# Moving the MLP's input in four transfers per block and by tokens in fours, with three reorderings around it, in a seven-product fp32 trunk

## What is computed

```python
def gmlp_mixer(h, w_in, ln_g, w_s, b_s, w_out):
    z = jax.nn.gelu(h @ w_in)
    u, v = jnp.split(z, 2, axis=-1)
    ...  # v is layer-normed; ws is w_s below its diagonal, per group of 256 columns
    sv = jnp.einsum('gts,bnsge->bntge', ws, v) + b_s.T[None, None, :, :, None]
    return (u * sv.reshape(b, l, GM_WIDTH)) @ w_out

def channel_mlp(h, w1, w2):
    return jnp.square(jax.nn.relu(h @ w1)) @ w2

x = x + gmlp_mixer(rms_norm(x, norm1_g), ...)
x = x + channel_mlp(rms_norm(x, norm2_g), mlp_w1, mlp_w2)
return rms_norm(x, final_g)
```

## Time and profile before

| what | value |
|---|---|
| median of three runs | 1123.8 us |
| the profiled execution's own time | 1123.38 us |
| its span, first to last instruction | 1121.3 us |
| TensorE busy | 1110.0 us, 99% of the span |
| VectorE busy | 796.9 us (71%) |
| ScalarE busy | 563.3 us (50%) |
| DMA | 195.9 MB, mean 175 GB/s |
| granted clock of TensorE | 0.999 of full speed |

### The profile page before, as it was taken

One profiled execution on the slowest core, in us unless ns is written; L12 is line 12 of the kernel. 1 busy time (PEld: TensorE's weight loads), 2 busy tenths in 40 slices (PEclk: granted clock), 3 DMA queues, 4 the chain that ended last, 5 costly groups with the idle time before them and its releaser, 6 DMA issues.

```text
span 1121.3 us, 13104 instructions
## 1 busy us (share of the span) xinstructions
PE 1110.0 (99%) x5050; PEld 922.8 (82%) x5050; DVE 796.9 (71%) x872; ACT 563.3 (50%) x870; POOL 23.0 (2%) x17
## 2 busy tenths in 40 slices
PE   9999999999999999999999999999999999999997
PEld 7888888888888888888788888888888888888886
DVE  5885656689779986699858447455598575677666
ACT  7764344554554434644674455454644333333456
POOL 0000000000000000000000000000000000000240
PEclk9999999999999999999999999999999999999999
DMA  9072353272875594643353635527878354343213
GB/s 333 16 222 106 107 181 109 93 256 81 319 256 196 186 351 153 191 122 103 114 187 144 194 113 191 196 102 272 301 292 298 121 217 188 113 151 113 78 73 150
DMA packets 86541, 195.90 MB, mean 175 GB/s; under 512 B 5048, under 2 KB 15312, under 8 KB 79824
## 3 DMA queue, kind: packets, MB, share of 16 engines
q1 hardware_dynamic: 85168, 194.28, 49.6%
q10 hardware_dynamic: 1312, 0.79, 0.3%
HBM read 134.23 MB, written 58.72 MB: 172 GB/s over the span
## 4 chain that ended last, share of the span: by engine, by line
PE 89%; DVE 7%; ACT 2%; issue 1%; DMA 1%; SPq 0%; DVEq 0%; ACTq 0%
PE banks L438 29%; PE banks L443 29%; PE banks L442 29%; PE banks L531 3%; DVE ring_low L1426 1%; DVE raw_a L1522 1%; DVE left_and_right L1462 1%; DMA left_and_right<-in_a_w_in_dram 1%; ACT ring_high L990 0%; DVE rows L1589 0%; DVE rows L1568 0%; ACT raw_a L1039 0%; DVE s_low L1512 0%; DVE raw_s L1555 0%; DVE pair_low L1434 0%
## 5 line engine op out<-in xcount | busy, mean ns | idle before, releaser
L1020 ACT ACTIVATE pair_high<-left_and_right 128x1024 fp32r<-128x1024 f32 x168 | 177.2, 1060 | 247.4 <-PE banks L438 199.5
L1426 DVE TENSOR_TENSOR ring_low<-left_and_right,ring_high 128x512 fp32r<-128x512 f32 x224 | 153.1, 693 | 186.0 <-ACT ring_high L990 185.3
L1434 DVE TENSOR_TENSOR pair_low<-left_and_right,pair_high 128x1024 fp32r<-128x1024 f32 x168 | 204.3, 1231 | 111.2 <-ACT pair_high L1020 111.2
L990 ACT ACTIVATE ring_high<-left_and_right 128x512 fp32r<-128x512 f32 x224 | 138.0, 628 | 254.6 <-PE banks L438 155.9
L438 PE MATMUL banks<-pair_high 128*128 128x512 f32 x672 | 262.0, 390 | 0.0
L442 PE MATMUL banks<-pair_low,pair_high 128*128 128x512 f32 x672 | 261.7, 389 | 0.0
L443 PE MATMUL banks<-pair_high,pair_low 128*128 128x512 f32 x672 | 261.7, 389 | 0.0
L438 PE MATMUL banks<-s_high,ring_high 128*128 128x512 f32 x384 | 150.0, 391 | 2.9 <-DVE s_low L1512 2.1
L442 PE MATMUL banks<-s_low,ring_high 128*128 128x512 f32 x384 | 149.6, 390 | 0.0
L443 PE MATMUL banks<-s_high,ring_low 128*128 128x512 f32 x384 | 149.5, 389 | 0.0
L438 PEld LDWEIGHTS banks<-pair_high 128*128 128x128 f32 x672 | 126.2, 188 | 26.4 <-DVE scratch L1616 0.3
(11 more groups left out here) (128 smaller groups left out, 1217.6 us busy)
## 6 DMA issues: line engine op xcount, KB each, us to landing
left_and_right<-sums SPq DMA_DIRECT2D x40, 1024.0 KB, 7.0
left_and_right<-in_mlp_w_dram SPq DMA_DIRECT2D x36, 1024.0 KB, 7.4
sums<-rows SPq DMA_DIRECT2D x34, 1024.0 KB, 5.3
left_and_right<-in_a_w_in_dram SPq DMA_DIRECT2D x19, 1024.0 KB, 7.3
v_blocks<-rows SPq DMA_DIRECT2D x8, 1024.0 KB, 4.5
left_and_right<-in_a_w_out_dram SPq DMA_DIRECT2D x8, 1024.0 KB, 10.0
rows<-in_x_dram SPq DMA_DIRECT2D x7, 1024.0 KB, 9.1
spare<-v_blocks SPq DMA_DIRECT2D x6, 1024.0 KB, 6.6
```

What stands on the lines that cost most here:

```text
L990: nc.scalar.activation(ring_high[k][:, :], right_place(n, pos)[:, k, :], ACT.Copy)\
L1020: nc.scalar.activation(pair_high[pair_entry(d, pos, k)][:, :, :], pair_of(d, pos, k), ACT.Copy)\
L1426: nc.vector.tensor_tensor(ring_low[k][:, :], right_place(n, pos)[:, k, :], ring_high[k][:, :].bitcast(F32), ALU.subtract).then_inc(low_don ...
L1434: nc.vector.tensor_tensor(pair_low[e][:, :, :], pair_of(d, pos, k), pair_high[e][:, :, :].bitcast(F32), ALU.subtract).then_inc(low_done, 1)
```

## The change

- **Moves.** `move_quads` now makes one transfer per quadrant: 32 partitions x 16 x 128 floats from 128 partitions x 4 x 128. Partition 4i + r, block m of the source lands in partition i's slot 4r + m, so the transposed token order is by fours: position p of tile r is token 4p + r of the block. All four blocks go straight from SBUF to SBUF, all on SP. The store of each block to DRAM stays (the residual is read back later) and now comes after the move.
- **Token order behind it.** Doubles 1 and 2 give rows by fours: the residual is loaded by fours (`y_fours`), the output is stored so (`out_v`), and `y_r2`, made at single 6 (`scale_y`), goes by DRAM into `y_r2_fours` with two small transfers at single 7. VectorE waits for the second at double 1, position 1.
- **Order on VectorE and ScalarE** between double 0, position 4, and single 4: transposes, splits and `add_rows` of the last two blocks change places (below). `high_turned("a12")` and `low_turned("a12")` stand ahead of the ring's first parts of single 4.
- **Start.** VectorE rounds k-tile 0 (`first_rounded`), and ScalarE begins with the first weight's high part.
- **First gelu.** The highs (4,0), (4,1) of single 0 stand ahead of `activate(0, "c11")`.

```diff
-        def move_quads(eng, b, blk, dst, quadrants):
-            for q in quadrants:
-                for r in range(4):
-                    eng.dma_start(dst[32 * q:32 * q + 32, r:4 * QT:4, :],
-                                  block_of[blk][32 * r:32 * r + 32, :, P * q:P * q + P]).then_inc(quads_landed[b], 16)
+        def move_quads(eng, b, blk, dst):
+            for q in range(4):
+                eng.dma_start(dst[32 * q:32 * q + 32, :, :], block_of[blk][:, :, P * q:P * q + P])\
+                  .then_inc(quads_landed[b], 16)
...
+                if n == 7:
+                    sp.wait_ge(y_step, 3)
+                    sp.dma_start(y_r2_dram.rearrange("m p -> p m"), y_r2[:, :], allow_slow_non_contiguous=True)\
+                      .then_inc(y_scales_stored, 16)
                 if kind(n) == "v" or kind(n) == "hid":
                     store_block(n, "c11")
...
                 if d == 0:
                     y_final(sp, "c12")
+                    move_quads(sp, "a11", "c12", quad_a11)
                     sp.dma_start(y_of("c12"), block_of["c12"]).then_inc(y_stored["c12"], 16)
                 left(11)
-                if d == 0:
-                    load_quads("a11", "c12", quad_a11)
                 left(12)
...
                 if d == 0:
                     y_final(sp, "c22")
+                    move_quads(sp, "a21", "c22", quad_a21)
                     sp.dma_start(y_of("c22"), block_of["c22"]).then_inc(y_stored["c22"], 16)
-                    load_quads("a21", "c22", quad_a21)
...
-                    move_quads(sp, "a22", "c21", quad_a22, (0, 1))
-                    sp.wait_ge(quads_landed["a22"], 256)
+                    move_quads(sp, "a22", "c21", quad_a22)
...
                 elif n == 4:
-                    high_turned("a12")
                     split_high(4, 1, 0)
-                    y_final(act, "c21")
-                    act.wait_ge(low_done, unit_double(0, 6, 7) + 1)
-                    move_quads(act, "a22", "c21", quad_a22, (2, 3))
                     split_high(4, 1, 1)
...
+                    split_high(0, 4, 0)
+                    split_high(0, 4, 1)
                     activate(0, "c11")
...
             act.wait_ge(eps_set, 1)
+            split_high(0, 0, 0)
             emptied(act, "g1", 7)
-            first_high(0)
-            split_high(0, 0, 0)
             first_high(1)
...
+            filled(dve, ("turn", 0, "a11"), 4)
+            nc.vector.tensor_scalar(high["a11"][:, 0, :], ps[:, 4, :], g1[:, 0:1], None, ALU.mult)\
+              .then_inc(first_rounded, 1)
             first_low(0)
```

More of the change, by code:

```diff
@@ L230, in trunk @@
         y_r2 = tiny("y_r2", [P, MT])
+        y_r2_fours = tiny("y_r2_fours", [P, MT])
         o_sq = tiny("o_sq", [P, 2, MT])
@@ L1591, in add_rows @@
                         nc.vector.scalar_tensor_tensor(
-                            out=piece, in0=ps[:, bank, :], scalar=y_r2[:, 4 * tb + m:4 * tb + m + 1], in1=piece,
+                            out=piece, in0=ps[:, bank, :], scalar=y_r2_fours[:, 4 * tb + m:4 * tb + m + 1], in1=piece,
                             op0=ALU.mult, op1=ALU.add).then_inc(drained[bank], 1)
@@ L1695, in single @@
                 elif n == 4:
-                    low_turned("a12")
                     split_low(4, 1, 0)
@@ L1699, in single @@
                     split_low(4, 1, 1)
-                    for k in range(2):
-                        turn_y("a22", [k])
-                        sum_turned("s2", [k])
+                    turn_y("a22", [0])
+                    sum_turned("s2", [0])
                     split_low(4, 1, 2)
+                    turn_y("a22", [1])
+                    sum_turned("s2", [1])
                     split_low(4, 1, 3)
@@ L1930, in double @@
                             sum_t_double(d, {1: 1, 2: 2, 4: 3}[pos], k - 4)
-                        if d == 0 and pos == 6:
-                            low_a11(4, k - 4)
-                        if d == 0 and pos == 6 and k in (5, 6):
-                            sum_turned("s3", [2 * k - 10, 2 * k - 9])
+                        if d == 0 and pos == 5 and k == 5:
+                            turn_y("a21", [0, 1])
+                        if d == 0 and pos == 5 and k == 6:
+                            turn_y("a21", [2, 3])
+                        if d == 0 and pos == 5 and k == 7:
+                            sum_turned("s3", [0, 1])
+                        if d == 0 and pos == 6 and k == 5:
+                            turn_y("a12", [0, 1])
+                        if d == 0 and pos == 6 and k == 6:
+                            turn_y("a12", [2, 3])
                         if d == 2 and pos == 6 and k == 5:
```

115 lines of the change are left out of this document (70 added, 45 removed).

## The result

The changed kernel takes **1139.3 us** (median of four, 1138.73 to 1140.08), against 1123.9 for the kernel before, timed beside it: ratio 1.0139, 95% interval 1.0119 to 1.0159. One of the four executions of the kernel before took 1395.8 us and is left out of the ratio. Slower by 15.4 us where no change was forecast, and far outside the range. The profiled execution took 1139.44 us, its span is 1137.5.

What follows compares the result with a forecast made beforehand. TensorE was taken as the bound. New waits of 4.0 us against the old 3.53 gave 0.5 slower: 1123.38 + 0.5 = 1123.9, its median 0.4 higher, so 1124.3 us, range 1120.7 to 1126.4.

Steps and rivals of the forecast that it cites:

- the length of a block's move: Each block's four transfers: 1.1 us ahead, 5.1 of bytes at 205 GB/s, 0.5 behind: 6.7 us, ends 5.0 and 7.4.
- The sum of the places: TensorE's waits from (5,6) to `s1`: 1.6 + 0.4 + 0.3 + 1.7 = 4.0 us against 3.53 before, 0.5 slower.
- (1), `c12`: Move issued right behind its row addition; its transposes come over the position after, so it is hidden at any speed.
- (2), `c22`: Block lands at 473.2 behind half 13; late transposes give a new wait of 1.6 us at (5,6), 0.4 at (5,7).
- The slope: A microsecond in a block's move is worth about 2.6 us, since it is paid at `c22` and again at `c21`.
- (3), `c11`: Single 4's first low part ready at about 504.4, TensorE wants it at 504.2: 0.3 us with the restart.
- (4), `c21` and `s1`: Block there at 514.2, `s1` starts at 538.8, due at 537.1: 1.7 us of the old 3.5 stay.
- The start: First matmul up to 0.5 us sooner, given back in the wait at 24.41: 0, ends -0.5 and +0.1.
- The gelu: First gelu: the bank copy still starts at 57.5, so TensorE's wait stays: 0, ends -0.3 and +0.1.
- The rest: Row scales' store at single 7 and tiny operations at single 6 cost nothing: 0, ends -0.1 and +0.2.
- B: Rival: `a21` lands from 473.9 on, late transposes push position 6's low parts too: +2.2, 1126.0, up to 1127; chance 0.13.
- A: Rival: moves quicker, a block in 5.1 us, new wait gone, nearly all of 3.5 us back: 1120.5; chance 0.21.

Runs made afterwards that it cites:

- quick moves: Changed kernel with every quadrant's transfer written onto all 128 partitions, leaving out the rearrangement, so it does not compute the layer; 1122.2 us, ratio 0.9976.
- transposes behind: Changed kernel with `a21`'s four transposes and the sums for `s3` back behind position 5's low parts; 1130.25 us, ratio 1.0038.
- and `c21` by pieces: Kernel of transposes behind, with `c21` moved by sixteen 64 KB pieces by tokens in fours, eight each on SP and ScalarE; 1126.1 us, ratio 1.0016.
- orders back: Changed kernel with VectorE's and ScalarE's order from double 0, position 4, to single 4 as before the change, `c21` by sixteen pieces on two queues; ratio 1.0016.
- mixture: Kernel of orders back, with `c21` moved by two whole quadrants and eight 64 KB pieces, one quadrant and four pieces per queue; ratio 1.0025.
- two queues: Changed kernel, orders kept, with `c22` and `c11` by four quadrants on two queues, `c22` ahead of half 13's load, `c21` by sixteen pieces; ratio 1.0073.
- half 13 behind: Changed kernel with `c22`'s four transfers ahead of the load of half 13, all still on SP; ratio 1.0087.
- start: Kernel before the change with only the start's and the first gelu's edits; ratio 1.0006.
- a finer wait at `s1`: Kernel before the change with the start and gelu edits, and `s1`'s first unit in single 4 waiting for its low part only before its last four matmuls; ratio 0.9987.

## Why the prediction was wrong, point by point

**The step that failed is the length of a block's move**, "I take 205 GB/s ... 6.7 us for a block". It measured 11.2 us for `c11` and 12.0 for `c21`. The even rate was taken from rows of the same destination but another source, and the SBUF-to-SBUF row was of transfers that the queue's issues had kept apart. The pieces of the sum: 5.1 us of bytes became 8.5 to 10.3, and 0.5 us behind the last became up to 1.4. Rows 6 had a sign of it: `c22`'s rate fell there too, from 353 to about 205 GB/s (and its thin rest is 20 to 28, not 33). I bounded the cost by the forms shown and not by the possibility that two ends together are worse than either. The upper end of 7.4 us was no bound: nothing in the trace of before showed 128 partitions of SBUF read into 32. The sum of the places, forecast and measured: (5,6) and (5,7) 2.0 and 7.7 us; lower clock 0 and 2.9; position 6 and single 4's start 0.3 and 2.2; from there to `s1` 1.7 and 7.2. That is 4.0 against 20.0, less the old 3.5 and 0.3 at the start: 16.2, the difference of the spans.

**(1), `c12`.** Held: its block took 11.8 us, VectorE waited 0.5 us for it, TensorE not at all.

**(2), `c22`.** "So a new wait of 1.6 us": right place, right releaser, and 7.7 us. Half 13's share was right: the first packet of the quads is at 467.4, forecast 467.6. But the bytes then took 10.3 us, not 5.1, and the block landed at 479.1 and not 473.2. With quick moves (landed 472.25) the same step gives 1.3 us for (5,6) and (5,7): the arithmetic held.

**The slope and the clock.** "A microsecond in a block's move is worth about 2.6 us" held: 4.5 (`c11`), 5.3 (`c21`) and 5.9 us (`c22`) more per block make 12 to 15, with the forecast's 0.5 some 12 to 16, and the spans have 13.3 without the lower clock. What the forecast had no term for is that lower clock behind a long wait, 2.9 us; with it the spans have 16.2. Behind the first 25 us no row of before had TensorE idle for more than 2.1 us, and I did not ask what more would bring.

**(3), `c11`.** "0.3 us with the restart": it was 2.2 us of delay at position 6 and single 4's start. The delay at (5,6) hid part of it; where that was mended, the first of these waits alone is 4.

**(4), `c21` and `s1`.** I had 24.6 us from VectorE's first transpose to `s1`. It is a constant:

| kernel | first issue of `c21` | first transpose | `s1` | difference | span |
|---|---|---|---|---|---|
| before | 506.55 | 513.58 | 538.35 | 24.77 | 1121.3 |
| after | 517.80 | 529.84 | 554.58 | 24.74 | 1137.5 |
| transposes behind | 507.91 | 519.71 | 544.47 | 24.76 | 1129.0 |
| and `c21` by pieces | 507.78 | 515.65 | 540.40 | 24.75 | 1123.4 |
| orders back | 506.64 | 515.73 | 540.49 | 24.76 | 1125.1 |
| mixture | 507.15 | 517.09 | 541.86 | 24.77 | 1126.4 |
| two queues | 510.57 | 519.26 | 544.02 | 24.76 | 1128.6 |
| half 13 behind | 513.03 | 524.89 | 549.62 | 24.73 | 1132.6 |
| quick moves | 505.50 | 512.35 | 537.09 | 24.74 | 1120.0 |

So the swap of orders there gains nothing, the landing of `c21` alone sets `s1`, and the forecast's 0.2 us for the swap was not there.

**The start.** "None of this moves, so that wait grows by what the start gained" is not so in the changed kernel's execution, where 0.34 us stay at 25 us, with VectorE's rows for the last transposes earlier too (24.11, before 24.41). But over the thirteen traces with these edits the median at 58 us is that of before, so a gain is not shown, and the forecast's 0 stands. **The gelu**: 0, as forecast: the copy's wait is 0.27 against 0.30. **The rest**: 0, as forecast. The scales took 19.3 us to land, and no wait came of them: behind `s1` both kernels take 582.9 us.

**Rivals.** B named the mechanism, late transposes of `a21` that push the low parts, and put its price at 2.2 us; it was its size by the move's true length, with the lower clock on top, that made 15.4. A needed a move that this form does not give; the run with quick moves shows what it would have been worth, 1.3 us by the spans and 2.7 by the timings of the hoped 3.3.

## What to carry to other kernels

A transfer has two ends, and a rate read from one that shares only the destination is no bound: measure the very pair of partition patterns before orders are built on its landing. If a step is moved ahead of work that feeds the busiest engine, it must be safe by the whole range of that landing; three moves as slow as these cost nothing where their users stood far behind, and over 10 us where two transposes stood in front of a low part. A matmul group that waits for one operand of three can be ordered so that the late one comes last.

## What the chip showed that I had not expected

- The fall of one transfer's rate on its own way: 290 GB/s for 0.7 us, then under 100, with spread sources and neighbouring destinations; 279 throughout if the destinations lie four apart. What lies behind it is open.
- TensorE's clock. After 7.5 us of idle time the granted clock was 0.51 for 6 us. The length of one wait does not tell it alone: it fell behind 2.27 us in the mixture's kernel and not behind 2.61 us in the one with two queues:

```profile
521.53 0.60 PE L452 MATMUL banks<-a_high,ring_high 128*128 128x512 f32 x1 [2.27 <-DVE ring_low L1447]
...
501.11 0.50 PE L452 MATMUL banks<-pair_high 128*128 128x512 f32 x1 [2.61 <-DVE pair_low L1464]
```

  Behind `s1`'s wait of 2.1 us, which comes after shorter ones, it fell in some executions and not in others, with nearly the same waits. The kernel with the start's edits alone (windows as above, of this stretch), where the matmuls from 538.0 to 541.5 start 0.43 us apart:

```profile
538.00:541.50 3.50, 3.50 (x8) 2.80 (x9) 2.71 (x3) 1.83 (x4) 0.00 (x0) 0.51 0.00 0
```

  and the kernel before, with waits of 0.31, 0.44 and 2.12 us there against 0.57, 0.44 and 2.13:

```profile
538.30:542.00 3.70, 3.65 (x16) 3.04 (x17) 2.92 (x3) 1.87 (x4) 0.00 (x0) 1.00 0.00 0
```

  It costs 1.6 us: from `s1` to the end the spans are 582.9 to 583.0 us without it (before, after, pieces, quick moves, half 13 behind) and 584.5 to 584.6 with it (transposes behind, orders back, mixture, two queues, start). That part of the spread of the kernel before, some 3 us, comes of it is likely, but only profiled executions show the clock.
- With `c21` by pieces on two queues, an issue on each at times takes much longer than 0.65 us, and both end together: 1.6 and 1.8 us (orders back), 1.7 and 1.8 (mixture), 1.3 and 1.6 (two queues), and with the old pieces of the kernel before 1.5 and 1.9 (a finer wait at `s1`). In the kernel before itself and in the first kernel with the new pieces none did. So it hangs on neither form, and it can be worth 1.5 us of `s1`, which makes it the second likely part of the spread; its cause is open.
